# The first expert of each layer takes its token rows from on-chip 0/1 matrices instead of a gather

## The reference, cut to what matters

```python
aff = jax.nn.softmax((xs @ router_w).astype(jnp.float32), axis=-1)
gate, idx = lax.top_k(aff.T, C)
xe = xs[idx]
he = jax.nn.silu(jnp.einsum('ecd,edf->ecf', xe, w1)) * jnp.einsum('ecd,edf->ecf', xe, w3)
ye = jnp.einsum('ecf,efd->ecd', he, w2) * gate[..., None].astype(h.dtype)
out = jnp.zeros_like(xs).at[idx.reshape(-1)].add(ye.reshape(-1, D))
```

## Time and profile before

| | |
|---|---|
| runs | 1943.24, 1949.09 and 1944.16 us, median 1944.16 |
| profiled execution | 1943.18 us, of which 1941.0 us from the first to the last instruction (span) |
| busy share of the span | PE 94%, DVE 80%, ACT 59%, POOL 16% |
| TensorE clock, mean granted share | 0.978 |
| read from HBM, rate over the span | 515.63 MB, 278 GB/s with the writes |
| chain that ended last | PE 84%, DVE 8%, transfers 3%; the expert products (L1169) alone 53% |

### The profile page before, as it was taken

One profiled execution on the slowest core, in us unless ns is written; L12 is line 12 of the kernel. 1 busy time (PEld: TensorE's weight loads), 2 busy tenths in 40 slices (PEclk: granted clock), 3 DMA queues, 4 the chain that ended last, 5 costly groups with the idle time before them and its releaser, 6 DMA issues.

```text
span 1941.0 us, 27033 instructions
## 1 busy us (share of the span) xinstructions
PE 1816.0 (94%) x9406; PEld 1268.2 (65%) x9406; DVE 1561.1 (80%) x2362; ACT 1154.5 (59%) x1545; POOL 302.6 (16%) x141
## 2 busy tenths in 40 slices
PE   3999888969999999999999998996999999999996
PEld 1777667846666666666667776784666666666663
DVE  4543767589999999999876376667899999999996
ACT  2410365248877777777652125623878777777773
POOL 0100030010222122221102003111022221222200
PEclk9999999979999999999999999997999999999998
DMA  9558201279999999999763722025999999999974
GB/s 341 181 209 312 104 9 45 98 281 419 391 389 382 387 365 389 382 384 381 282 203 133 261 67 88 23 105 200 426 382 387 381 390 374 375 375 388 387 295 160
DMA packets 86602, 540.12 MB, mean 278 GB/s; under 512 B 6928, under 2 KB 12050, under 8 KB 61956
## 3 DMA queue, kind: packets, MB, share of 16 engines
q1 hardware_dynamic: 76036, 502.54, 66.3%
q0 software_dynamic: 10496, 36.64, 6.9%
HBM read 515.63 MB, written 23.53 MB: 278 GB/s over the span
## 4 chain that ended last, share of the span: by engine, by line
PE 84%; DVE 8%; DMA 3%; issue 2%; ACT 2%; POOL 1%; SPq 0%; DVEq 0%; ACTq 0%; POOLq 0%
PE bank L1169 53%; PE bank L842 10%; PE bank L1029 5%; PE bank L718 2%; DMA ring<-in_exp_w 1%; PE bank L1186 1%; PE bank L988 1%; PE bank L1050 1%; PE bank L1179 1%; PE bank L1067 1%; DMA ring<-in_ada_w 1%; PE bank L973 1%; PE bank L877 1%; DVE arena_u L1874 1%; PE bank L1100 1%
## 5 line engine op out<-in xcount | busy, mean ns | idle before, releaser
L1470 ACT ACTIVATE arena_h_r<-ring 128x1024 fp32r<-128x1024 f32 x480 | 503.4, 1060 | 170.2 <-PE bank L1169 150.6
L2076 DVE TENSOR_TENSOR ring_r<-ring,arena_h_r 128x1024 fp32r<-128x1024 f32 x470 | 557.2, 1219 | 29.5 <-ACT arena_h_r L1470 22.6
L1169 PE MATMUL bank<-arena_h_r,arena_u_r 128*80 128x512 f32 x1280 | 374.1, 399 | 10.1 <-DVE arena_u_r L2096 10.1
L2076 DVE TENSOR_TENSOR ring_r<-ring,arena_u_r 128x1024 fp32r<-128x1024 f32 x282 | 333.9, 1222 | 13.2 <-ACT arena_u_r L1470 6.7
L1470 ACT ACTIVATE arena_u_r<-ring 128x1024 fp32r<-128x1024 f32 x288 | 300.4, 1058 | 59.5 <-PE bank L1169 59.5
L1169 PE MATMUL bank<-ring_r,arena_u_r 128*80 128x512 f32 x1024 | 319.2, 393 | 0.0
L1169 PEld LDWEIGHTS bank<-arena_h_r,arena_u_r 128*80 128x80 f32 x1280 | 188.8, 152 | 106.2 <-DVE arena_u_r L2096 7.8
L1169 PE MATMUL bank<-arena_u_r 128*80 128x512 f32 x768 | 216.9, 391 | 0.0
L1169 PEld LDWEIGHTS bank<-ring_r,arena_u_r 128*80 128x80 f32 x1024 | 152.4, 149 | 85.3 <-issue 1.8
L1169 PE MATMUL bank<-arena_h_r,arena_z_r 128*80 128x512 f32 x640 | 181.1, 397 | 3.6 <-DVE arena_z_r L2111 3.6
L670 POOL DMA_INDIRECT arena_z<-xn_dram,icur x32 | 133.8, 4182 | 308.5 <-issue 277.4
(11 more groups left out here) (302 smaller groups left out, 2604.1 us busy)
## 6 DMA issues: line engine op xcount, KB each, us to landing
ring<-in_exp_w SPq DMA_DIRECT2D x192, 2048.0 KB, 10.3
ring<-in_ada_w SPq DMA_DIRECT2D x24, 2048.0 KB, 8.8
ring<-in_w_in SPq DMA_DIRECT2D x8, 2048.0 KB, 18.1
ring<-in_w_out SPq DMA_DIRECT2D x2, 4096.0 KB, 12.7
x_res<-arena_z POOLq DMA_DIRECT2D x10, 512.0 KB, 3.4
xn_dram<-arena_u POOLq DMA_DIRECT2D x10, 512.0 KB, 3.0
arena_z<-x_res POOLq DMA_DIRECT2D x5, 512.0 KB, 4.6
arena_z<-in_x_sample SPq DMA_DIRECT2D x4, 512.0 KB, 6.5
```

Of the source, the lines that this page charges most:

```text
L1169: mm = pe.matmul(bank[out + n][0:CAP, :], xs[:, c, :], w[:, n * 512:(n + 1) * 512], start=(c == 0 and part == 0), stop=(c == KC - 1 and pa ...
L1470: act.activation(high[c], slot[s][:, c, :], ACT.Copy).then_inc(high_ready, 1)
L2076: v.tensor_tensor(slot_r[s][:, c, :], slot[s][:, c, :], high[c], ALU.subtract).then_inc(low_ready, 1)
```

## The change

For expert 0 of each layer no rows are gathered. Its list becomes two 0/1 matrices on DVE: `first_list` copies the merged list of expert 0 over 128 columns, one small PE product turns it, so that every partition holds the 64 row numbers, and `first_picks` compares these with the number of the token that the partition stands for (`token_at`, four new columns of the constant `sel`, and a fifth for the context tokens, `picks_ctx`). PE then multiplies each 128-column piece of `xn`, which is still in SBUF, by these matrices (`picked`), which gives the rows of expert 0 already turned, in banks 6 and 7. The rest of the row work is done in two halves of four chunks (`first_rows`, `first_rows_rest`, result in `heT`). SP's wait for the gathers is gone: w3(0) and the first half of w2(0) start when `xn_dram` is written. The first gather is now that of expert 1.

In the lists, the two copies from bank 7 and the copy of the context affinities are left out (the first round reads PSUM), ACT instead of DVE writes `xn` of tile 4, and the maximum of tile 4's logits stands ahead of `lists_cast`. ACT rounds chunks 5 to 7 of w1(0) after the picks, because those buffers share memory with `xn`. Experts 0 and 1 stand ahead of the loop, and `rows(1)` stands between w3(0) and w1(1).

```diff
-                        if s == 1 and before is None and not h:
-                            for u in range(2):
-                                sp.wait_ge(xe_in[u], l * (PAIRS * 16) + 16)
-                        elif before is None:
+                        if before is None:
                             sp.wait_ge(wo_mm, l * NT + NT)
...
                 fill(1, "exp_w3", 0, None)
+                fill(2, "exp_w2", 0, None, (0,))
                 fill(0, "exp_w1", 1, 0)
-                fill(2, "exp_w2", 0, None)
+                fill(2, "exp_w2", 0, None, (1,))
...
+                pe.matmul(bank[3][:, 0:CAP_L], first_list, ident[0:CAP_L, 0:CAP_L], start=True, stop=True).then_inc(top_mm, 1)
+
+                def picked(t, c):
+
+                    at = c % 4 * CAP + (CAP_L if t == NT - 1 else 0)
+                    m, which = (CAP_C, picks_ctx) if t == NT - 1 else (CAP_L, picks[:, t, :])
+                    return pe.matmul(bank[6 + c // 4][:, at:at + m], xn[:, t, c:D:KC], which,
+                                     start=(t in (0, NT - 1)), stop=(t in (3, NT - 1)))
+
+                pe.wait_ge(top_done, l * 6 + 4)
+                for c in range(4):
+                    for t in range(4):
+                        picked(t, c)
+                pe.wait_ge(top_done, l * 6 + 5)
+                pe.matmul(bank[3][:, CAP_L:CAP], ones_row, topf[0:1, CAP_L:CAP], start=True, stop=True)
...
+                pe.wait_ge(top_done, l * 6 + 6)
+                for c in range(4):
+                    mm = picked(NT - 1, c)
+                mm.then_inc(top_mm, 1)
+                for c in range(4, KC):
+                    for t in range(NT):
+                        mm = picked(t, c)
+                mm.then_inc(xeT_mm, 1)
...
                 pe.wait_ge(top_out, l + 1)
-                rows_T(0, 0)
-                pe.wait_ge(xeT_out, l * EXPERTS + 1)
-                product(0, 0, 0, xeT[0])
-                with pe.Fori(0, PAIRS - 1) as k:
+                product(0, 0, 0, heT)
+                expert(0, 0, 0, x=heT)
+                expert(1, 1, 0)
+                with pe.Fori(1, PAIRS - 1) as k:
...
+                def first_rows():
+
+                    act.wait_ge(x1_out, l * 80 + 80)
+                    for n in range(2):
+                        c = slice(4 * n, 4 * n + 4)
+                        act.wait_ge(xt_done, l * (EXPERTS + 1) + n + 1)
+                        act.activation(heT[0][:, c, :], xt[:, c, :], ACT.Copy).then_inc(xh_done, 1)
+                    act.wait_ge(xn_out, l * 80 + 80)
+                    act.wait_ge(xeT_mm, l * EXPERTS + 1)
...
                     if turn == 3:
-                        normed2(4)
+                        last_inverse2()
...
-                for c in range(4):
-                    first_rest(c)
-                rows(0, 0)
-                rows_rest(0, 0)
-                for c in range(4, KC):
+                first_rest(0)
+                first_rows(0)
+                first_rest(1)
+                first_rows_rest(0)
+                first_rows(1)
+                first_rest(2)
+                first_rows_rest(1)
+                for c in range(3, KC):
                     first_rest(c)
                 rest(w3_at(0), 1)
-                with v.Fori(0, PAIRS - 1) as k:
+                rows(1, 1)
+                rest(w1_next_at(0), 0, {1: lambda: rows_rest(1, 1)})
+                hidden(0)
```

More of the change, by code:

```diff
@@ L200, in hybrid_prefix_diffusion_step @@
         affC = [sflat[0:EXPERTS, a:a + CTX] for a in (512, 1920)]
+        picks = sflat[:, 0:4 * CAP_L].rearrange("p (t s) -> p t s", t=4)
+        picks_ctx = sflat[:, 4 * CAP_L:4 * CAP_L + CAP_C]
+        first_list = sflat[0:CAP_L, 384:384 + P]
         turn = sflat[:, 2208:2208 + P]
@@ L582, in _, with fill @@
                 sp.dma_start(slot[2], i["w_out"][l].rearrange("(c p) n -> p c n", p=P)).then_inc(wo_in, 16)
-                def fill(s, name, e, before):
-                    for h in range(2):
-                        if s == 1 and before is None and not h:
-                            for u in range(2):
-                                sp.wait_ge(xe_in[u], l * (PAIRS * 16) + 16)
-                        elif before is None:
+                def fill(s, name, e, before, halves=(0, 1)):
+                    for h in halves:
+                        if before is None:
                             sp.wait_ge(wo_mm, l * NT + NT)
@@ L1188, in hidden_T, with expert @@
                     mm.then_inc(heT_mm, 1)
-                def expert(e, u, k, last=False):
-                    product(w3_at(e), 1, 2, xeT[u], (None, None) if last else (1, lambda: rows_T(1 - u, k + u)))
+                def expert(e, u, k, last=False, x=None):
+                    product(w3_at(e), 1, 2, xeT[u] if x is None else x, (None, None) if last else (1, lambda: rows_T(1 - u, k + u)))
                     if last:
@@ L1504, in prepare @@
                     rounded(w3_at(e + 1), 1, e + 1)
-                with act.Fori(0, PAIRS - 1) as k:
+                rounded(w1_next_at(0), 0, 1, (1, lambda: rows(1)))
+                rounded(w2_at(0), 2, 0, (3, lambda: hidden(0)))
+                gated(w1_next_at(0), 1)
+                rounded(w3_at(1), 1, 1)
+                u = 1
+                prepare(1)
+                with act.Fori(1, PAIRS - 1) as k:
                     for u in range(2):
@@ L2039, in _ @@
                 v.wait_ge(affT_mm, l * 2 + 1)
[L2040 to L2042 removed]
                 for turn in range(CAP_L // 8):
[L2044 removed]
+                    top_round(turn, affL if turn else (bank[7][0:TWO, 0:LHALF], affL[1]), slice(0, TWO), 0, CAP_L)
                     if turn == 1:
@@ L2254, in tables @@
     c["consts"] = m
-    s = np.zeros((P, 2 * P + CAP))
+    s = np.zeros((P, 2 * P + CAP + NT))
+    s[:, 2 * P + CAP:] = np.arange(P)[:, None] + P * np.arange(NT)[None, :]
     for n in range(2):
```

86 lines of the change are left out of this document (60 added, 26 removed).

## The result

The changed kernel took 1956.20 us (median of six runs), the kernel before 1943.43 (median of six): ratio 1.0071, interval 1.0056 to 1.0086. It is slower by about 13 us, where 1939.0 (range 1934.5 to 1946) was forecast.

The account below looks back on a forecast made before the run. PE was taken to bound the loop, DVE the entry to each layer's expert part. Gains of 1.9 and 3.9 us in the two layers, less 1.6 for a cold stretch, gave -4.2 on 1943.18: 1939.0 us, range 1934.5 to 1946.

Parts of the forecast that it names:

- Lists: Lists ahead of the picks, layer 0: DVE starts 0.67 us earlier, 0.5 counted; PE picks from about 407.2.
- Picks: 80 pick instructions on PE, layer 0: 0.11 us each at 2.4 GHz, 0.17 at 1.2, ending at about 418.8.
- no load time of its own: Picks on PE: weight loads lie under matmuls as in the loop, so nothing is added for them.
- Clock: PE during the picks: back at 2.4 GHz after 4 us of small matmuls.
- The Trainium skill's rule on loads: Loads overlap a running matmul only in different row groups; a pick's columns would come on top, 1946.2 us; chance 0.03.
- DVE behind the picks: DVE from the picks' end to hidden(0): 30.4 us without waiting for weights, ending at 449.2 in layer 0.
- What is late next: PE ahead of turning the hidden rows: idles about 1.8 us per layer; one cold stretch counted, +1.6 us.
- the slow rival: Picks at 1.2 GHz, first product starts cold, PE (28.6 us and 2 more) sets the turning; 1944.5 to 1948.1, chance 0.14.
- The picks drag: Picks at 1.2 GHz throughout, 0.17 to 0.19 us each, end at 422.2 to 424.0; 1944.5 to 1948.1 us, chance 0.14.
- picks that end 2.9 us later than I say: Sign at the end of PE's picks: from this delay on, both layers' gains are used up.

Follow-up runs that it names:

- contiguous_warm: Changed kernel with picks reading 128 adjacent columns of xn and five filler matmuls on PE ahead of the picks; 1947.22 us, one run.
- warm_ahead: Changed kernel with five filler matmuls in PE's gaps ahead of the picks; 1962.69 us, ratio 1.0108.
- Swapped: Changed kernel with the picks' operands swapped: 0/1 matrix as weight, xn passing with 512 columns, 20 instructions in place of 80; 1950.18 us, ratio 1.0032.
- half_permuted: Kernel before with the first half of w3(0) ahead of the gathers and xn stored so that PE's turnings of it read adjacent columns; 1933.60 us, ratio 0.9942.

## Why the prediction was wrong, point by point

**Lists.** Right: the first pick was forecast 407.2 - 389.54 = 17.7 us behind the filler's start, and stands at 405.24 - 387.52 = 17.7.

**Picks.** The step that failed: "eight in 1.04 us, which less 0.17 for the pipe's end is 0.11 each", with 0.13 to 0.19 as bounds at 1.2 GHz, and "I take 4" us until the clock is back. A pick instruction measured 0.24 us and the clock stayed at 0.50 to their end, so the 80 took 19.5 us where I had 10.3 (4.0 + 1.0 + 0.9 + 4.4), and ended 20.45 us after the first (405.24 to 425.69) instead of 11.6. Nor did "no load time of its own" hold: the load, 336 ns where those of the nearest transposes are 191 (median of the kernel before), set the pace. The transposes that I took as nearest do read the same pieces of `xn`, but are another kind of instruction; what I gave as a bound was none. The contiguous_warm run shows that 0.115 is the price of such a pick with adjacent columns at 2.4 GHz: right number, wrong access.

**Clock.** The step was wrong and nothing hung on it alone: warm_ahead shows 0.24 at 1.00 as well. With adjacent columns it would have decided between 0.115 and 0.22.

**The Trainium skill's rule on loads.** Not borne out: with 64 columns an instruction took 0.115 us in contiguous_warm, with 16 columns the router's took 0.12, so the columns did not come on top. What the prediction left out here is that the load itself can set the pace of the instructions.

**DVE behind the picks.** Right: 30.4 us forecast, 425.89 to 455.98 is 30.1, with no wait for weights. The gathers of expert 1 were not late either.

**What is late next.** The 1.8 us of PE waiting ahead of the hidden rows became 0.68 in layer 0 and none in layer 1, since the first product started at 1.2 GHz: 1399.10 - 1368.18 is 30.9, the 28.6 and 2 of the slow rival.

**The rivals.** "The picks drag" is what came, at its place; its price of 0.17 to 0.19 was too low, and so was the time it gave, 1944.5 to 1948.1. It was to decide "from picks that end 2.9 us later than I say": they ended 8.9 later (20.45 less 11.6), and 8.9 less 2.9, twice, is 12.0, against 12.3 measured in the entries.

## What to carry to other kernels

Price an instruction by a row that has the same kind, the same step of reading and the same clock, not by one that reads the same tensor; where two of the three differ, test the largest count of instructions at double the price before believing a gain. A wait in a queue's list may be there for the transfer of another queue: fill the idle time in front of it instead of removing it. And ask of each operand that PE reads in steps whether its writer could store it in the order of reading; here that was worth more in the two loops (8 us) than the change was forecast to give (4.2).

## What the runs showed of the hardware that I had not expected

- Weights of 128x128 float32 read in steps of eight elements (32 bytes) took 0.24 us per instruction at either clock, with adjacent columns 0.115 at 2.4 GHz and 0.22 at 1.2. The Trainium skill, "Advanced Engine Details and Errata", section "Memory Cachelines", says that SBUF works in lines of 16 bytes and that an access to another line each time costs; a step of 32 bytes does that, and the runs agree. The turning of 80 gathered rows shows the same, 1.01 against 0.72 us. It also reached the writers, which must then do the step: ACT 2.14 us for 1.15, DVE 1.21 for 0.75.
- The Trainium skill, "TensorE: Matmul & The Clock Gate", section "LDWEIGHTS (loading the stationary operand)", gives a load as its columns divided by 1.2, in ns, which makes an estimate of 107 for 128. With adjacent columns at 2.4 GHz the picks followed each other in 115, near it, while one load of theirs takes 192; at 1.2 GHz and in steps of eight the spacing was about twice as long.
- Picks kept PE busy for 20 us and the granted clock stayed at 0.50; in contiguous_warm it fell from 1.00 to 0.50 while picks ran. Swapped, with 512 columns per load, the clock rose in the course of the picks.
- The transposes in steps of eight suffer less than the picks: 0.13 us each (at 364.18), with loads of 191 ns, and 140 with adjacent columns in half_permuted, where the loads of picks go from 335 to 192 at 1.00. Why was not tried; so 0.24 is shown for the picks, not for every operand in steps.
